# A two-stack mixer network on one core: the roots of the feed-forward norms move from VectorE to ScalarE

## The reference

```python
def _rmsnorm(x, w):
    y = x * lax.rsqrt(jnp.mean(x * x, axis=-1, keepdims=True) + 1e-6)
    return y * w
def _swiglu(h, w_gate, w_up, w_down):           # 1024 -> 2816 -> 1024
    return (jax.nn.silu(h @ w_gate) * (h @ w_up)) @ w_down
# first stack:  x = x + 0.5 * _swiglu(_rmsnorm(x, ffn_norm), ...)
# second stack: the same without 0.5, and a causal convolution of
#               three taps on h @ w_gate ahead of silu
```

## Time and profile before

| | us |
|---|---|
| median of 3 runs | 2291.45 (2290.14 to 2293.19) |
| the profiled execution, its own time | 2288.56 |
| its span, first to last instruction | 2286.8 |
| PE busy | 2151.7 (94%) |
| POOL busy | 1521.6 (67%) |
| ACT busy | 1015.7 (44%) |
| DVE busy | 998.4 (44%) |

### The profile page before, as it was taken

The page is one execution under the profiler, slowest core; times in us unless marked ns, Lnnn a source line. Parts: engine busy times, 40 slices in busy tenths (PEclk is TensorE's granted clock), DMA queues, the critical chain, the costliest instruction groups (busy, mean ns, idle before and its releaser), DMA issues.

```text
span 2286.8 us, 39306 instructions
## 1 busy us (share of the span) xinstructions
PE 2151.7 (94%) x14719; PEld 1951.9 (85%) x14719; DVE 998.4 (44%) x1727; ACT 1015.7 (44%) x1458; POOL 1521.6 (67%) x664
## 2 busy tenths in 40 slices
PE   6999998989999999998989996999899989998999
PEld 6997778979988997777979986989799878998997
DVE  3451366443403452366333403453577025444860
ACT  4443416434444443425444433436444344355442
POOL 5787424537886787525438885757588866576896
PEclk9999999999999999998999998999999999999999
DMA  6755313015555655313025564434355544344553
GB/s 210 216 182 184 108 60 111 1 56 169 184 188 165 214 178 172 111 57 110 1 74 178 183 225 132 149 116 161 129 185 185 196 142 156 111 166 130 185 185 129
DMA packets 250736, 331.19 MB, mean 145 GB/s; under 512 B 9024, under 2 KB 224938, under 8 KB 250026
## 3 DMA queue, kind: packets, MB, share of 16 engines
q1 hardware_dynamic: 250074, 326.19, 44.0%
q0 software_dynamic: 464, 2.37, 0.3%
HBM read 327.48 MB, written 1.05 MB: 144 GB/s over the span
## 4 chain that ended last, share of the span: by engine, by line
POOL 42%; issue 32%; PE 22%; ACT 2%; DVE 2%; POOLq 0%; DMA 0%; ACTq 0%; DVEq 0%
POOL w_lo L855 40%; PE psB L397 3%; PE psB L399 3%; PE psB L398 3%; PE psA L397 3%; PE psA L398 3%; PE psA L399 3%; PE psA L1595 2%; PE psB L1618 1%; PE psB L1625 1%; POOL Mm_even L847 1%; POOL Mm_odd L847 1%; PE psA L1710 1%; POOLq L854 0%; DVE MT L1181 0%
## 5 line engine op out<-in xcount | busy, mean ns | idle before, releaser
L855 POOL TENSOR_TENSOR w_lo<-raw,w_hi 128x1024 fp32r<-128x1024 f32 x600 | 1452.1, 2439 | 697.9 <-ACT w_hi L545 697.3
L397 PE MATMUL psA<-xT_hi,w_lo 128*128 128x256 f32 x3296 | 954.7, 290 | 48.5 <-POOL w_lo L855 19.4
L398 PE MATMUL psA<-xT_lo,w_hi 128*128 128x256 f32 x3296 | 941.1, 286 | 0.0
L399 PE MATMUL psA<-xT_hi,w_hi 128*128 128x256 f32 x3296 | 940.9, 285 | 0.0
L545 ACT ACTIVATE w_hi<-raw 128x1024 fp32r<-128x1024 f32 x600 | 629.0, 1051 | 389.2 <-PE psB L399 238.2
L397 PEld LDWEIGHTS psA<-xT_hi,w_lo 128*128 128x128 f32 x3296 | 641.4, 195 | 62.2 <-issue 26.9
L398 PEld LDWEIGHTS psA<-xT_lo,w_hi 128*128 128x128 f32 x3296 | 641.2, 195 | 2.9 <-issue 2.9
L399 PEld LDWEIGHTS psA<-xT_hi,w_hi 128*128 128x128 f32 x3296 | 641.0, 194 | 0.0
L978 DVE TENSOR_TENSOR hT_lo<-hfull,hT_hi 128x256 fp32r<-128x256 f32 x132 | 237.1, 1828 | 7.8 <-ACT hT_hi L602 7.1
L397 PE MATMUL psB<-w_hi,hT_lo 128*128 128x512 f32 x528 | 209.1, 396 | 0.5 <-POOL w_lo L855 0.5
L399 PE MATMUL psB<-w_hi,hT_hi 128*128 128x512 f32 x528 | 208.8, 395 | 0.0
(11 more groups left out here) (379 smaller groups left out, 2349.4 us busy)
## 6 DMA issues: line engine op xcount, KB each, us to landing
raw<-in_w_in SPq DMA_DIRECT2D x78, 1024.0 KB, 5.3
raw<-in_ffn_w_gate SPq DMA_DIRECT2D x44, 1024.0 KB, 5.3
raw<-in_ffn_w_up SPq DMA_DIRECT2D x44, 1024.0 KB, 5.3
raw<-in_ffn_w_down SPq DMA_DIRECT2D x44, 1024.0 KB, 4.9
raw<-in_w_ffn_in SPq DMA_DIRECT2D x44, 1024.0 KB, 5.1
raw<-in_w_ffn_out SPq DMA_DIRECT2D x22, 1024.0 KB, 4.8
raw<-in_w_out SPq DMA_DIRECT2D x16, 1024.0 KB, 4.9
raw<-in_w_branch_da SPq DMA_DIRECT2D x4, 1024.0 KB, 5.2
```

What stands on the lines that cost most here:

```text
L397: nc.tensor.matmul(o, a_lo, b_hi, start=start, stop=False, skip_group_check=skip)
L398: nc.tensor.matmul(o, a_hi, b_lo, start=False, stop=False, skip_group_check=skip)
L399: return nc.tensor.matmul(o, a_hi, b_hi, start=False, stop=stop, skip_group_check=skip)
L855: nc.gpsimd.tensor_tensor(split_half(w_lo, n, kind), raw_half(n, kind), split_half(w_hi, n, kind).bitcast(F32), ALU.subtract)\
```

## The change

The sums of squares themselves are spread over the partitions, and the roots are made behind that, by ACT: root = exp(-0.5 ln(ss/1024 + eps)), once on the row (`root_row`, 128x256) and once on the two columns (`out_scale`, 128x2). DVE's `inverse_root` goes out of `norm_gained` (it stays in `norm_scale` for the other norms). The factor 0.5 of the first stack is multiplied in by DVE at pass j = 2. On PE the spreading matmuls stand behind half s0+1 instead of behind s0+2. On ACT the diagonals come first, then the roundings of pass 0 (halves s0+3 to s0+6) stand among the steps of the root, ahead of the first silu. Two small activations on one column load the tables of Ln and of Silu early.

```diff
-            def root_across(st, l, f):
-                act.wait_ge(root_ready[st].sem, root_ready[st].due(l, f + 1))
+            def root_across(st, l, q):
+                act.wait_ge(n_ss[st].sem, n_ss[st].due(l, 2 * q + 2))
                 for rb in range(RB):
-                    ins_ = A(diag[:, rb, :], ident, ACT.Copy, scale=rstd[:, rb:rb + 1])
+                    ins_ = A(diag[:, rb, :], ident, ACT.Copy, scale=ss[:, rb:rb + 1])
                 ins_.then_inc(root_diag[st].sem, 1)
+            def roots(st, l, f):
+                ch = act_chain[st]
+                act.wait_ge(root_mm[st].sem, root_mm[st].due(l, f + 1))
+                A(root_row[:, :], psB[:, 0, 0:L], ACT.Ln, scale=1.0 / D, bias=eps)
+                A(out_scale, ss, ACT.Ln, scale=1.0 / D, bias=eps).then_inc(ch.sem, 1)
+                act.wait_ge(ch.sem, ch.step(l))
+                A(root_row[:, :], root_row[:, :], ACT.Exp, scale=-0.5).then_inc(root_out[st].sem, 1)
+                A(out_scale, out_scale, ACT.Exp, scale=-0.5).then_inc(root_cols[st].sem, 1)
...
                 for j in range(NF // 2):
                     for i in range(2):
                         n = 2 * j + i
-                        round_half(st, l, s0 + 4 * j + i + AHEAD)
                         if n == 0:
-                            root_across(st, l, f)
-                            act.wait_ge(root_mm[st].sem, root_mm[st].due(l, f + 1))
-                            A(root_row[:, :], psB[:, 0, 0:L], ACT.Copy).then_inc(root_out[st].sem, 1)
+                            root_across(st, l, 2 * f if st == 0 else 1)
+                            round_half(st, l, s0 + AHEAD)
+                            A(stat[:, 47:48], eps, ACT.Ln, bias=eps)
+                            round_half(st, l, s0 + 1 + AHEAD)
+                            roots(st, l, f)
+                            round_half(st, l, s0 + 2 + AHEAD)
+                            A(stat[:, 47:48], eps, ACT.Silu)
+                            round_half(st, l, s0 + 3 + AHEAD)
+                        if j:
+                            round_half(st, l, s0 + 4 * j + i + AHEAD)
...
-                        round_half(st, l, s0 + 4 * j + 2 + i + AHEAD)
+                        if j:
+                            round_half(st, l, s0 + 4 * j + 2 + i + AHEAD)
...  (VectorE, norm_gained)
-                dve.wait_ge(n_ss[st].sem, n_ss[st].due(l, 2 * q + 2))
-                inverse_root(l, dve_chain[st], rstd, ss, 1.0 / D)
-                V.tensor_scalar(out_scale, rstd, scale, None, ALU.mult).then_inc(root_ready[st].sem, 1)
...  (VectorE, ffn)
                     if j == 2:
+                        if st == 0:
+                            dve.wait_ge(root_cols[0].sem, root_cols[0].due(l, f + 1))
+                            V.tensor_scalar(out_scale, out_scale, 0.5, None, ALU.mult).then_inc(ch.sem, 1)
+                            dve.wait_ge(ch.sem, ch.step(l))
+                        else:
+                            dve.wait_ge(root_cols[1].sem, root_cols[1].due(l, 1))
...  (TensorE, ffn)
                         project_T(st, l, s0 + 4 * j + i, psA[:, i, 0:L], q if j == 0 and i == 0 else None)
+                        if j == 0 and i == 1:
+                            root_across(st, l, f)
...
                         project_T(st, l, s0 + 4 * j + 2 + i, psA[:, 2 + i, 0:L])
-                        if j == 0 and i == 0:
-                            root_across(st, l, f)
```

More of the change, by code:

```diff
@@ L329, in emit @@
         gain_chosen = pair("gain_chosen", 2, 1, start=1)
-        root_ready = pair("root_ready", 2, 1)
+        root_cols = pair("root_cols", 2, 1)
         root_diag = pair("root_diag", 2, 1)
@@ L898, in norm_rest, with norm_gained @@
                                     ALU.subtract).then_inc(n_lo[st].sem, 1)
-            def norm_gained(st, l, q, f, scale):
+            def norm_gained(st, l, q):
                 for i in range(4):
@@ L1431, in _ @@
             with dve.Fori(0, DEPTH) as l:
-                norm_gained(0, l, 0, 0, 0.5)
+                norm_gained(0, l, 0)
                 ffn(0, l, 0, 0)
@@ L1440, in _ @@
                 add_to_x(0, l, 1, 101, 1.0)
-                norm_gained(0, l, 2, 1, 0.5)
+                norm_gained(0, l, 2)
                 ffn(0, l, 1, 102)
@@ L1458, in _ @@
                 add_to_x(1, l, 0, 65, 1.0)
-                norm_gained(1, l, 1, 0, 1.0)
+                norm_gained(1, l, 1)
                 ffn(1, l, 0, 66)
```

## The result

| | before | after |
|---|---|---|
| median of the runs made side by side, us | 2292.32 (2290.14 to 2296.41, 4 runs) | 2264.42 (2264.28 to 2268.85, 4 runs) |
| the profiled execution's own time | 2288.56 | 2264.50 |
| its span | 2286.8 | 2262.7 |

The ratio is 0.9884, with an interval of 0.9868 to 0.990: the changed kernel is faster by 27.9 us between the medians, and by 24.1 us between the two profiled executions. The forecast was 28.5 us less and 2263.0.

What follows compares the result with a forecast made beforehand. PE, busy 94%, bounds the kernel and loses 28.5 us at six FFN heads: 18.9 in gaps, 9.6 in slow clock. Less that, the median 2291.45 becomes 2263.0 us; the forecast's own range is 2258 to 2268.

Steps and rivals of the forecast that it cites:

- The gap is gone: At each FFN head, PE's idle gap ahead of half s0+4 goes, with 3.4 us to spare; gaps total 18.9 us.
- Spare times: At the 508 us head, POOL's lead over PE: 3.4, 2.3, 2.6, 2.7 us for s0+4 to s0+7.
- from there the steady order of before holds: Behind s0+7 in the head, the kernel before's regular order continues; spare at s0+7 is 2.7 us.
- Row ready about 1 us earlier: At the heads, `root_row` is ready about 1 us earlier relative to the spreading's old place: 517.1 against 518.0.
- 12 more loads, each followed at once: ACT gets 12 more table loads in the heads, 15.4 us in all, each costing 1.28 us and no more.
- Rival 3: Something of a load's size, 1.3 us more, stands around each table load in ACT's heads; 2271 us; chance 5%.
- The clock comes back: Behind the head gaps, PE's granted clock returns to 1.00; the slow clock's part is 9.6 us.
- rival 1: At the heads the gap goes but the slow clock stays, having another cause; gain 18.9, 2272.5 us; chance 12%.
- Rival 2: In the two FFNs that fetch parameters, DMAs hold it up; about 2.1 us lost in each, 2267 us; chance 8%.
- SP's issues move with the halves: On SP's queue, the argument against the DMA rival, Rival 2: issues follow `lo_done` and come earlier with it.
- Up to 5 us, if the other seven waits for POOL go too.: PE's seven waits for POOL besides the six head gaps, 5.3 us together, might go too: up to 5 us more.
- Rivals 4 and 5: 4: roundings in heads need loads of their own, 2291 us, 5%. 5: ACT's longer head stalls for instructions, 2320 us, 4%.

Runs made afterwards that it cites:

- e1: Kernel before with DVE's roots kept and only ACT's order of roundings changed: 2266.97 us, ratio 0.9887.
- e2: Changed kernel with ACT's roots, but the roundings of s0+4 to s0+6 back in their old places behind them: 2279.75 us, ratio 0.995.
- e8: Changed kernel with four more squares on ACT, each waiting for the one before, between the roots and the rounding of s0+5: 2283.57 us, ratio 0.996.
- e3: Kernel before with 13 matmuls of no use ahead of pass j = 1 of each FFN, filling PE's gap: 2284.71 us, ratio 0.997.
- e4: Changed kernel with the DMA of the next norm's gain issued at pass 7 of the FFN instead of pass 4: 2258.93 us, ratio 0.9855.
- e10: Kernel before with DVE's roots, the roundings moved ahead and the next norm's gain loaded at pass 7: 2266.75 us, ratio 0.9895.
- e6: Changed kernel with the rounding of s0+6 behind the second rounding of the result instead of ahead of the first silu: 2263.62 us, ratio 0.9866.
- e7: Changed kernel with both the later rounding of s0+6 and the next norm's gain loaded at pass 7: 2264.87 us, ratio 0.9866.
- e4b: Changed kernel with the next norm's gain loaded at pass 7, run again in the third group: 2258.1 us, ratio 0.9853.
- e9: Changed kernel without the two tiny activations that load the tables of Ln and Silu early: 2262.98 us, ratio 0.9872.

## Why the prediction came out right, step by step

The mechanism was the forecast one, and the number came out nearer than the forecast deserved. The heads gave 29.5 us, 1.0 more than the sum. Some 6 were lost in the two FFNs that fetch parameters, which the sum had put at nothing, and 3.5 were won in a mixer, which it had not seen. That these partly cancel is luck.

- **"The gap is gone" at s0+4.** Right, in all six heads. The rounding of s0+4 ended 4.2 us behind the start of the diagonals (505.78 to 509.99), as forecast (510.2 to 514.4). That the gap was made by ACT's order is shown by e1 (gone, with DVE's roots kept) and e2 (1.95 to 2.65 us left, with ACT's roots).
- **Spare times.** Between POOL's end with a half and PE's start on it, the changed kernel's head has 3.2 us at s0+4, 2.5 at s0+5 (e8 says the same), 2.9 at s0+6 and 3.3 at s0+7. Forecast were 3.4, 2.3, 2.6 and 2.7. But "from there the steady order of before holds" was wrong: at s0+8 the spare is 1.6, and POOL works in bursts until 552 us, 45 us behind its first half of the head, with idle times of 1.20, 2.09 and 2.10 us between.
- **Row ready about 1 us earlier.** Right: 512.56 lies 3.04 us behind the spreading (509.52), which itself stands one half, 2.88 us, earlier. Counted from the old place that is 0.16, where before it was 518.00 - 516.96 = 1.04. Ln and Exp were taken at 0.47 and 0.41 and measured 0.48 and 0.42.
- **12 more loads, each followed at once.** Right. ACT's groups in the changed kernel (busy us, mean ns, idle before):

```profile
L600 ACT ACT_TABLE_LOAD x6 | 7.7, 1283 | 0.1
```

  Two more lines (584, 604) read the same, 18 loads of 1283 ns, where there were 6. Behind each, ACT goes on within 0.02 us (507.45 + 1.28 = 508.73, next at 508.74; 512.13 and 512.14; 514.90 and 514.91). Rival 3 falls. The drain of about 1380 ns that the Trainium skill puts beside each switch (ScalarE: Activation LUTs, section "What ACT_TABLE_LOAD costs") isn't in this trace; its 1283 ns for the load itself agree exactly.
- **The clock comes back.** Right, and e3 shows that it hangs on PE's standing still, so rival 1 falls. The terms were 4.37 for each head of the first stack, 4.94 and 6.04 for the second; the undisturbed four measured 4.4, 4.4, 5.7 and 6.8. Of the 0.8 more in each of the second stack, 0.4 to 0.5 is a short wait for POOL that went (0.21 and 0.19 us idle, ahead of 1726.49 and 2173.58 in the kernel before), and the rest lies in the head. The two gaps of the second stack were equal and their slow stretches not, which had spoken for rival 1: behind the one the granted clock was 0.50 from 1656.80 to 1660.20, behind the other from 2100.50 to 2107.30.
- **Rival 2, the DMAs.** This is the term that was mis-sized: the sum had nothing lost in the two FFNs with parameters, and I gave 8% to a loss of 2.1 us in each. They lost 2.4 and 3.6, 6.0 together, but only 3.4 of it is late weights (0.9 in the first, 1.3 and 1.15 in the third). The rest, 1.6 at the start of the first and 1.3 at the start of the third, is a later start, a longer slow pace and a low stretch of the clock. I had seen a rounding wait 1.83 us for its data and held that "SP's issues move with the halves". They did, but into other traffic: the gain's issue took 4.30 us instead of 2.56, and ACT then waited 5.33 for its unit. e4 takes 2.7 us off the third FFN by moving that one DMA. It isn't the DMA alone, though: in e1 and e10 PE is as early, and with the gain at pass 4 or at pass 7 the third FFN takes 198.1. Nor does the length of that issue decide: in e3 it took 1.60 and ACT waited 3.42, in e6 4.20 and ACT waited 1.74.
- **"Up to 5 us, if the other seven waits for POOL go too."** They did not go: 5.3 us in 7 waits before, 7.7 in 7 after, 3.5 of them at the three places named above.
- **Not in the forecast:** 3.5 us in the mixer of the last layer, from DVE's second stand in its norm. That stand is absent in every kernel of this study that has the roots on ACT (a `xn` wait of 25.6 to 26.3) and present in every one that keeps them on DVE (29.1: before, e1, e3, e10). Which instruction of the changed code moves it isn't known.
- Rivals 4 and 5 fall: no rounding in a head has a load of its own, and no stand for "issue" lies in a head. There is the one of 3.12 us at the start of a loop's second pass, as before, and a new one of 4.49 ahead of 1815.05, at the end of the fifth FFN, which cost nothing: that FFN takes 192.2 us as the sixth does.

So the sum held by its large terms, and was 4.4 us too high in the traces: 28.5, less 6.0 in two FFNs, plus 1.6 in the others, and mixers that add up to nothing, is 24.1. The medians lie 27.9 apart here and 32.4 and 31.6 in the other two groups, on both sides of the forecast; a mixer alone varies by 5.4 us between executions of the changed kernel (280.3 to 285.7), so a difference of 4 between traces and medians is of that size.

**What stays open.** Why the weights come late in the FFNs with parameters. At 783 us DVE works on the parameters' small network, `gs` comes at 779.02 and POOL stands idle for 3.94 us ahead of 780.91. The wait there is 1.47 to 1.71 us in the changed kernel, 1.71 in e6, 1.12 in e7, and 0.42 or none in e4b and e4. It is also there with DVE's roots, when only idle matmuls are put in (e3: 1.20, and 1.41 in the first FFN). Over the traces it goes with POOL's bursts behind the head. In the two FFNs with parameters of the kernel before, of e1 and of e10, POOL works half by half again from 34 us behind the FFN's start or sooner, and no such wait is over 0.38 us. In all others the bursts behind the head last until 51 us or more, and each has a wait of 0.9 to 1.7 us in one of the two FFNs or both, except e4 (0.33 at most). That goes together in 14 traces and isn't shown as a cause; no run changed the bursts alone. Why the later gain cures the wait by itself and not together with the later rounding, no run shows either.

## What to carry to other kernels

When the engine that sets the time stands still, ask first which instruction of the feeding engine is waiting in line behind something it does not need: here three roundings behind a root made the whole gap, and moving them gave 25 us without touching the arithmetic. Try that move alone first: here the new arithmetic on top of it won in four FFNs about what those with parameters then lost. Lay the new order out with the durations of the trace, and keep the spare time of each step, for that is what an experiment can check. And price separately the stages that share their queue with other traffic: a DMA issued in a crowd can hold up the one behind it that is needed. Set the two traces side by side instruction by instruction before you name a cause; of the 6.0 us here, half was a late start and the clock.

## What the runs showed of the hardware

- **A short stand of TensorE can cost its clock for half as long again.** With 2.7 us idle the granted clock fell behind the gap (0.79 over 8 us) in four heads of four. With 1.95 us it fell once in four (e2), with 2.65 both times, with 1.77 twice in six (e8: 0.86 behind two, 1.00 behind four), and with the gap filled by idle matmuls it fell in none of the six heads (e3). Ahead of the third FFN it fell behind 2.33 us (the changed kernel) and did not behind 2.40 (before). Equal gaps need not cost the same.
- **Small DVE instructions beside POOL.** 2-element instructions on SBUF took 2.33 and 2.35 us instead of 0.16 while POOL subtracted 128x1024, and `hT_lo` 4.07 us for two instead of 0.97; instructions that read a block from PSUM kept to 0.42 beside the same POOL work (hfull at 524.71, POOL busy from 523.19). The Trainium skill (SBUF — State Buffer, "Who interferes with whom") says that an instruction of VectorE with two inputs in SBUF contends with one of GpSimd that reads SBUF, over a port pair that they share by an exclusive lock. The traces agree, with the 2.33 us above.
- **Table loads don't wait.** In e9 a load (1.28 us, done at 507.68) ran ahead of its activation's wait, which ended at 508.19, so a dummy activation to preload a table bought nothing there.
- **The issue of a DMA has no fixed price on SP's queue.** In the third FFN the same DMA of a gain took 0.43 us to issue at pass 7 (e4), and from 1.60 (e3) over 2.56 (before) to 4.30 (the changed kernel) at pass 4, behind those of the parameters. In the first FFN it took 1.11 there in the changed kernel.
